# Modulation in chunks of two channel tiles, with the first head's projections and gates formed tile by tile between them

## The chip, the cores and the metric

The kernel runs on one core of one Trainium2 chip. The metric is device time in microseconds (us) of one execution; a kernel's time is the median of its runs. Engines are named as in the profile: PE (TensorE), PEld (its weight loads), DVE (VectorE), ACT (ScalarE), POOL (GpSimd) and SP (SyncE, which here only issues DMAs).

## The reference, cut to what matters

One layer of a hybrid trunk over 128 context tokens and 1024 latent tokens (1152 in all, nine token tiles of 128), with 1024 channels (eight channel tiles of 128). What the change touches is the beginning:

```python
shift, scale, gate = jnp.split(silu(c) @ w_mod + b_mod, 3, axis=-1)   # c_ctx for the context tokens, c for the latents
h = rmsnorm(x, p['norm_w']) * (1 + scale) + shift
proj = h @ p['w_in']
qkv, z_a, x_b, z_b, gate_cols = jnp.split(proj, [OFF_QKV, OFF_ZA, OFF_XB, OFF_ZB], axis=-1)
q, k, v = l2norm(...silu(conv(qkv))...)                                # 8 heads of 128
alpha_f, beta_f, alpha_b, beta_b = jnp.split(gate_cols, 4, axis=-1)    # 32 columns
g = -exp(a_log) * softplus(alpha + dt_bias);  beta = sigmoid(beta)     # both directions
# then per head: chunked gated delta rule in both directions, RG-LRU branch, merge, output projection
```

(The first line is shortened from the model code that feeds the layer; the rest is the reference's.) All products have float32 accuracy. For the large ones the kernel splits each operand into a high and a low part of type fp32r and adds three products (high by high, high by low, low by high).

## The kernel before, in words

The program is written engine by engine, by hand; semaphores alone order the engines, and each engine works its own list strictly in order. `front_stage` (L153 on) holds everything up to the end of the eight DeltaNet heads, `tail_stage` the rest. The change touches `front_stage` alone, before and just inside head 0.

**x and modulation.** For each of nine token tiles t, SP loads x (L337, `x_load`, three buffers, so a load waits until tile t-3 is normalised), ACT squares it with a row sum (L649), POOL forms the reciprocal root (L450, L452), ACT scales it (L643), PE transposes it in eight blocks into two PSUM banks (L893 to L896), and DVE copies it to `xt`, channels on partitions (L1205). Between the transposes of tiles 0 to 7, PE forms the modulation: silu(c) for channel tile t (128 x 2, the stationary operand) by 2048 columns of `w_mod` (the moving one), four matmuls per t (L881), summed over t in four PSUM banks. So shift and scale exist only after all eight. Then DVE copies the four 2x512 rows out (L1210), PE transposes them (L900), DVE forms `gain` and `shift` for all eight channel tiles (L1217 to L1220), and the modulated rows begin.

**Rows and the first block.** For each channel tile k, DVE writes x * gain + shift (L1233), ACT rounds it to the high part (L660), DVE subtracts for the low part (L1226). PE, in step with k, forms the first 128-column block of `w_in` (the key of head 0): three token groups of 384 columns by three products, nine matmuls per k (L912, L913, L917), and the 32 gate columns: again nine matmuls per k, with the 128x32 gate weights stationary and 384 tokens moving (L922, recorded as L124 to L126). The gates thus come out with columns on partitions; ACT copies them out (L663) and PE turns them with nine small transposes (L928).

**The second and third block, and the gates.** PE then forms blocks 1 (query) and 2 (value) of head 0 with `project(j, g)` (L848), 24 matmuls for each of three groups. Among them stand the gate transposes, the cumulative sums of the decays (L940) and the turning of their results (L947). DVE works the gates (L1241 to L1277), starts the convolutions of head 0 (`conv`, L1146 and L1148, one multiply and three multiply-adds per row), and copies the decay rows out (L1280); SP stores them and loads them back broadcast over the partitions (L322, `decay_in`); POOL masks them (L467); ACT takes their exponential (L612). Between two convolutions DVE forms the rate of the other branch (`softplus` of lambda and two scalings, L1282 to L1285).

**Head 0.** PE begins with the sums of squares of q (L963, after ACT's `square_q`, L607), turns the key (L864), and forms the key products (L970), the last two groups after ACT has copied the key out (L714). DVE needs the row sums of ACT's squares (L710) before it goes on (L1294), and from there runs to the end of the triangular solve (L1341, L1343, 31 steps, L1353); ACT then places blocks (L761), for which PE's L1032 waits. The projections of the next head are placed by hand between PE's steps.

**Filler.** `keep_busy` (L129) issues matmuls whose result nobody reads: 9 at the start (L875), 23 before the first block (L902), 10 before head 0 (L952).

The weights go through one staging buffer `wst` (`load(j)`, L316), ACT's `high(j)` and POOL's `low(j)` make the two parts, and `load(j)` waits until the low part of block j-1 is done.

## Time and profile before

| | us |
|---|---|
| median of 3 runs | 1642.02 |
| lowest and highest | 1639.0, 1642.07 |
| profiled execution, its own time | 1642.41 |
| its span in the trace | 1640.6 |
| PE busy in the span | 1591.3 (97%) |
| DVE, ACT, POOL busy | 1001.6, 805.4, 348.2 |
| mean granted TensorE clock | 0.992 of full |

Busy PE time comes from records whose ends are modelled: a matmul of 384 columns shows 335 ns, but the next starts about 173 ns later. The pace is therefore read from starts. A matmul of two float32 operands leaves two records.

### The profile page before, as it was taken

To read this page: it belongs to the slowest core of one execution; us is meant where nothing else is said; L and a number is where in the kernel's file an instruction comes from. 1 tells how busy PE (TensorE), PEld (TensorE's weight loads), DVE (VectorE), ACT (ScalarE), POOL (GpSimd) and SP (SyncE) were. 2 spreads that over 40 slices of the span, in tenths; PEclk is the share of its full clock that TensorE was granted. 3 is DMA by queue.
4 is the path that set the end of the run, shared out by engine and by line. 5 is a ranking of instruction groups with operands and counts; after the bars stand their busy time and mean duration, and the time that the engine had idled before them with its cause. 6 is when DMAs were issued, how large, how long until landed. Compare 5 with 4: busy or idle time off the path is not lost. (4 is left out here: it accounts for less than half of the span.)

```text
span 1640.6 us, 25151 instructions
## 1 busy us (share of the span) xinstructions
PE 1591.3 (97%) x9994; PEld 1512.5 (92%) x9994; DVE 1001.6 (61%) x1729; ACT 805.4 (49%) x1655; POOL 348.2 (21%) x272
## 2 busy tenths in 40 slices
PE   8989999999999999999999999999999999999997
PEld 3789999999999999999969999999999999999886
DVE  2647869597786959778664475663574641244444
ACT  4336474655748465564724764566466630221211
POOL 1122322121232212122211222221221211143110
PEclk9999999999999999999999999999999999999999
DMA  9121112012221201212240121212122262344123
GB/s 322 54 61 27 72 30 95 21 41 71 57 72 30 96 20 41 72 57 71 69 137 17 47 77 51 79 55 74 53 75 60 75 199 74 102 153 136 54 77 128
DMA packets 115855, 127.27 MB, mean 78 GB/s; under 512 B 6461, under 2 KB 97430, under 8 KB 115738
## 3 DMA queue, kind: packets, MB, share of 16 engines
q1 hardware_dynamic: 115594, 125.60, 23.8%
q8 instruction: 79, 1.29, 0.3%
q14 instruction: 38, 0.31, 0.1%
q10 hardware_dynamic: 144, 0.07, 0.0%
HBM read 105.56 MB, written 20.09 MB: 77 GB/s over the span
## 5 line engine op out<-in xcount | busy, mean ns | idle before, releaser
L124 PE MATMUL mb<-h_hi,w_hi 128*128 128x384 f32 x1088 | 365.3, 336 | 6.8 <-PEq L156 3.4
L125 PE MATMUL mb<-h_lo,w_hi 128*128 128x384 f32 x1088 | 364.7, 335 | 0.0
L126 PE MATMUL mb<-h_hi,w_lo 128*128 128x384 f32 x1088 | 364.5, 335 | 0.0
L124 PE MATMUL db<-h_hi,w_hi 128*128 128x384 f32 x808 | 283.6, 351 | 4.9 <-ACT padded_rows L668 2.2
L126 PE MATMUL db<-h_hi,w_lo 128*128 128x384 f32 x808 | 271.4, 336 | 0.0
L125 PE MATMUL db<-h_lo,w_hi 128*128 128x384 f32 x808 | 271.4, 336 | 0.0
L1665 POOL TENSOR_TENSOR w_lo<-w,w_hi 128x1024 fp32r<-128x1024 f32 x47 | 126.9, 2702 | 475.2 <-ACT w_hi L1692 475.2
L124 PEld LDWEIGHTS mb<-h_hi,w_hi 128*128 128x128 f32 x1088 | 205.1, 188 | 8.3 <-issue 4.7
L125 PEld LDWEIGHTS mb<-h_lo,w_hi 128*128 128x128 f32 x1088 | 205.1, 189 | 0.0
L126 PEld LDWEIGHTS mb<-h_hi,w_lo 128*128 128x128 f32 x1088 | 205.1, 189 | 0.0
L124 PEld LDWEIGHTS db<-h_hi,w_hi 128*128 128x128 f32 x808 | 152.9, 189 | 5.8 <-ACT d_kq L663 2.6
L125 PEld LDWEIGHTS db<-h_lo,w_hi 128*128 128x128 f32 x808 | 153.1, 189 | 0.0
L126 PEld LDWEIGHTS db<-h_hi,w_lo 128*128 128x128 f32 x808 | 152.4, 189 | 0.0
L1692 ACT ACTIVATE w_hi<-w 128x1024 fp32r<-128x1024 f32 x47 | 49.6, 1058 | 122.0 <-PE mb L126 76.5
L1938 DVE SCALAR_TENSOR_TENSOR l_tg<-l_tg,d_dt 128x1155 f32<-128x1155 f32 x16 | 36.5, 2324 | 96.4 <-ACT l_tg L1759 96.4
L811 ACT ACTIVATE d_vn<-db,d_nc 128x128 f32<-128x128 f32 x144 | 45.0, 363 | 96.8 <-DVE d_vk L1403 94.0
L1343 DVE TENSOR_TENSOR d_qg<-d_qg 128x31 f32<-128x31 f32 (+15 forms) x248 | 85.2, 344 | 8.5
L1341 DVE TENSOR_TENSOR d_qg<-d_qg 128x31 f32<-128x31 f32 (+15 forms) x248 | 84.6, 341 | 7.3
L1042 PEld LDWEIGHTS db<-d_w,d_u 128*96 128x96 f32 x864 | 77.1, 165 | 0.3
L1042 PE MATMUL db<-d_w,d_u 128*96 128x32 f32 (+2 forms) x864 | 76.7, 248 | 0.0
L518 POOL COPY d_w<-d_qg 32x288 f32<-32x288 f32 x32 | 22.6, 707 | 225.2 <-DVE d_qg L1353 223.8
L460 POOL TENSOR_TENSOR w_lo<-w,w_hi 128x1024 fp32r<-128x1024 f32 x20 | 47.6, 2380 | 102.8 <-ACT w_hi L542 102.8
(303 smaller groups left out, 2955.8 us busy)
## 6 DMA issues: line engine op xcount, KB each, us to landing
w<-in_w_in SPq DMA_DIRECT2D x48, 512.0 KB, 4.0
d_dt<-decay_rows SPq DMA_DIRECT2D x16, 576.0 KB, 5.5
d_qg<-decay_rows SPq DMA_DIRECT2D x16, 512.0 KB, 7.6
w<-in_w_gate SPq DMA_DIRECT2D x16, 512.0 KB, 3.9
branch_a<-d_kq SPq DMA_DIRECT2D x8, 576.0 KB, 3.2
branch_b<-l_z SPq DMA_DIRECT2D x8, 576.0 KB, 2.8
merge_gates_b<-l_gates SPq DMA_DIRECT2D x8, 576.0 KB, 5.2
m_in<-merge_gates_b SPq DMA_DIRECT2D x8, 576.0 KB, 3.8
```

What stands on the lines that cost most here:

```text
L124: pe.matmul(out, hi, rhi, start=(k == 0), stop=False)
L125: pe.matmul(out, hi, rlo, start=False, stop=False)
L126: return pe.matmul(out, lo, rhi, start=False, stop=(last and stop))
L460: pool.tensor_tensor(wlo[:, j % 2], wst[:, :, :], whi[:, j % 2].bitcast(F32), ALU.subtract).then_inc(S["w_lo"], 1)
L518: pool.tensor_copy(dst[bs, ns, bs], src_[bs, :].rearrange("p (b n) -> p n b", n=B)[:, ns, :]).then_inc(S[sem], 1)
L811: act.activation(vn[:, d, :], bank[3 + 2 * d][:, 0:P], ACT.Copy, scale=ncol[:, d, t:t + 1]).then_inc(S["vn"], 1)
L1042: mm = pe.matmul(back_bank(level, d, p)[0:3 * B, (t - t0) * width:(t - t0 + 1) * width], umat[:, d * NT + t, rc[d]], vinv(d, t)[:, col:col ...
L1341: link(dve.tensor_tensor(prod, amat[:, k * B + k + 1:(k + 1) * B].unsqueeze(2).broadcast_to([P, n, m]), xmat[:, k * B:k * B + m].unsqueeze ...
L1343: link(dve.tensor_tensor(low_rows, low_rows, prod, ALU.add))
L1665: pool.tensor_tensor(wlo_of(item), wst[:, slot(j)], whi_of(item).bitcast(F32), ALU.subtract).then_inc(S["w_lo"], 1)
L1692: act.activation(whi_of(item), wst[:, slot(j)], ACT.Copy).then_inc(S["w_hi"], 1)
L1938: dve.scalar_tensor_tensor(out=tg[:, 2 * d + 1, :], in0=tg[:, 2 * d + 1, :], scalar=1.0, in1=xc, op0=ALU.add, op1=ALU.mult).then_inc(S["p" ...
```

## The change: what it does

- The modulation is formed in four chunks; chunk c gives shift and scale for channel tiles 2c and 2c+1 alone. It sums over all eight input tiles, 256 + 256 columns of `w_mod` for each, eight matmuls per chunk. `w_mod` comes in 32 DMAs of 256 KB into eight buffers. Chunk 0 is formed between the transposes of token tiles 3 to 6, chunk 1 after those of tile 8, chunk 2 after channel tile 1, chunk 3 after channel tile 3. Each chunk has one row copy, four small transposes and three small DVE operations of its own.
- Between the chunks, for each channel tile, PE forms blocks 0 and 1 of `w_in` together (18 matmuls of 384 columns) and the gates.
- The gates are formed by tokens: for each of nine token tiles the 128x128 tile of h is stationary and the 128x32 gate weights move, three products each, 27 matmuls per channel tile, straight into the layout that the nine transposes made before. Those and ACT's copy go.
- DVE reads the gates after the last channel tile; block 1 is by then done, and only block 2 is left among the cumulative sums.
- x has four buffers; all four loads go out first, and the other loads are in a new order. The first block's weights are rounded during tile 5, their low part comes from DVE after tile 6. Block 2's weights have buffers of their own.
- The `softplus` of lambda moves into head 0, ahead of the transposes of the solve.
- `keep_busy` and its three uses are gone. Before head 0 PE waits for the copy of the decay rows.

The diff, cut to its core:

```diff
-        x = (flat_of(w1)[:, 0:D], flat_of(w1)[:, D:2 * D], flat_of(w2)[:, 0:D])
+        x = (flat_of(w1)[:, 0:D], flat_of(w1)[:, D:2 * D], flat_of(w2)[:, 0:D], flat_of(w2)[:, D:2 * D])
...
@@ SP
-            x_load(0)
-            x_load(1)
+            for t in range(NX):
+                x_load(t)
             sp.wait_ge(S["rows_zero"], 1)
...
+            for c, r, src, n in sources[0:9]:
+                sp.dma_start(rows_in_[r:r + n, c, :], src).then_inc(S["rows_in"], 16)
+            mod_load(0, 0)
+            x_load(4)
+            mod_load(0, 1)
...
+            load(0)
+            x_load(5)
+            mod_load(0, 2)
...
+            x_load(8)
+            mod_load(1, 1)
+            load(1)
+            mod_load(1, 2)
+            mod_load(1, 3)
...
+            for q in range(PARTS):
+                mod_load(2, q)
             load(2)
+            for q in range(PARTS):
+                mod_load(3, q)
             load(3)
...
@@ PE
-            keep_busy(pe, bank[7][:, 0:P], ident, 9)
             pe.wait_ge(S["silu_c"], 1)
+
+            def modulation(c, q):
+                n = c % 2 * PARTS + q
+                pe.wait_ge(S[f"wm{n}"], 32 * (c // 2 + 1))
+                if q == 0 and c >= 2:
+                    pe.wait_ge(S["mod"], 3 * c)
+                for k in range(2):
+                    mm = pe.matmul(bank[0 if c == 1 else 1][0:2, :], sc[:, :, 2 * q + k],
+                                   wmod[n][:, k].rearrange("p a n -> p (a n)"), start=(q == 0 and k == 0),
+                                   stop=(q == PARTS - 1 and k == 1))
+                mm.then_inc(S["mod_part"], 1)
...
+                if 3 <= t < 7:
+                    modulation(0, t - 3)
+                elif t == 7:
+                    mod_turned(0)
+            for q in range(PARTS):
+                modulation(1, q)
             pe.wait_ge(S["x_e"], NT)
-            pe.wait_ge(S["mod"], 2)
             pe.wait_ge(S["par_done"], 1)
...
+            pe.wait_ge(S["mod_row"], 2)
+
+            def first_blocks(k):
+                pe.wait_ge(S["h_hi"], k + 1)
+                for j in range(2):
+                    low_done(pe, j)
+                    for g in range(NG):
...
+                        pe.matmul(b[:, 0:GW], whi[:, j, k, :], R.hhi[:, k, ts], start=(k == 0), stop=False)
+                        pe.matmul(b[:, 0:GW], wlo[:, j, k, :], R.hhi[:, k, ts], start=False, stop=False)
+                pe.wait_ge(S["h_lo"], k + 1)
...
+                for t in range(NT):
+                    ts = slice(t * P, (t + 1) * P)
+                    at = bank[0][:, t * 4 * H:(t + 1) * 4 * H]
+                    pe.matmul(at, R.hhi[:, k, ts], wghi[:, k, :], start=(k == 0 and t == 0), stop=False,
+                              skip_group_check=True)
+                    pe.matmul(at, R.hhi[:, k, ts], wglo[:, k, :], start=False, stop=False, skip_group_check=True)
+                    mm = pe.matmul(at, R.hlo[:, k, ts], wghi[:, k, :], start=False, stop=(k == KT - 1),
+                                   skip_group_check=True)
+                return mm
+
             for k in range(KT):
-                pe.wait_ge(S["h_hi"], k + 1)
...
+                mm = first_blocks(k)
+                if k % 2 == 0 and k < KT - 2:
+                    mod_turned(k // 2 + 1)
+                elif k in (1, 3):
+                    for q in range(PARTS):
+                        modulation(k // 2 + 2, q)
             mm.then_inc(S["g_mm"], 1)
-            pe.wait_ge(S["g_row"], NG)
-            project(1, 0)
...
-            project(1, 1)
-            project(1, 2)
+            project(2, 0)
             pe.wait_ge(S["consts_in"], 16 * len(consts))
             pe.wait_ge(S["gates_raw"], 3)
...
-            project(2, 0)
+            project(2, 1)
             pe.wait_ge(S["cum_exp"], 2)
...
-            project(2, 1)
             project(2, 2)
-            keep_busy(pe, bank[5][:, 0:P], ident, 10)
+            pe.wait_ge(S["dec_copy"], 1)
             pe.wait_ge(S["cum_exp"], 4)
@@ DVE
+                if t == 6:
+                    dve.wait_ge(S["w_hi"], 1)
+                    dve.tensor_tensor(wlo[:, 0], wst[:, :, :], whi[:, 0].bitcast(F32), ALU.subtract).then_inc(S["w_lo"], 1)
+                elif t == 7:
+                    gains(0)
...
-                if k:
+                if k % 2:
+                    if k == 1:
+                        mod_rows(1)
                     low_rows(k - 1)
-            low_rows(KT - 1)
-
-            dve.wait_ge(S["g_t"], 1)
+                    low_rows(k)
+                    if k < KT - 1:
+                        if k > 1:
+                            mod_rows(k // 2 + 1)
+                        gains(k // 2 + 1)
+
+            dve.wait_ge(S["g_mm"], 1)
...
             conv(0, 2, range(TAPS))
-            softplus(sct[:, :], lu[:, :], lw[:, :], lr[:, :], ll[:, :], lam, -1.0)
...
             conv(0, 1, range(TAPS))
...
                 link(ins)
+                if h == 0:
+                    softplus(sct[:, :], lu[:, :], lw[:, :], lr[:, :], ll[:, :], lam, -1.0)
...
                 dve.wait_ge(S["u"], (h + 1) * 2 * NG)
```

`mod_rows(c)` waits for the chunk's last matmul and copies its 2x512 row; `mod_turned(c)` is four small transposes of it; `gains(c)` forms gain and shift for two channel tiles.

## Rows read from the trace of the kernel before

**Rows 1.** The page: the span, and its busy times by engine.
```profile
span 1640.6 us, 25151 instructions
PE 1591.3 (97%) x9994; PEld 1512.5 (92%) x9994; DVE 1001.6 (61%) x1729; ACT 805.4 (49%) x1655; POOL 348.2 (21%) x272
```

**Rows 2.** Timeline, 0 to 62 us: start, duration, engine, line, instruction, count.
```profile
3.04 4.21 PE L132 MATMUL db<-ident 128*128 128x128 f32 x18
...
18.56 1.09 PE L894 MATMUL db<-ident,d_dt 128*128 128x128 f32 x8
...
19.58 1.88 PE L881 MATMUL db<-d_kn,silu_c 128*2 128x512 f32 x4
...
50.59 2.46 DVE L1210 COPY d_k<-db 2x512 f32<-2x512 f32 x4
50.73 1.09 PE L894 MATMUL db<-ident,d_w 128*128 128x128 f32 x8 [1.45 <-DVE xt L1205]
...
61.67 0.42 PE L912 MATMUL db<-h_hi,w_hi 128*128 128x384 f32 x1
```

**Rows 3.** Groups by line, ACT, first 130 us: busy, mean ns, idle before, releaser.
```profile
L649 ACT ACTIVATE d_u<-d_w 128x1024 f32<-128x1024 f32 x9 | 9.5, 1057 | 23.2 <-DMA d_w<-in_x_sample 21.9 <-DMA d_w<-in_x_prompt 1.3
L643 ACT ACTIVATE d_w<-d_w,rstd 128x1024 f32<-128x1024 f32 x5 | 5.7, 1135 | 0.0
```

**Rows 4.** Busy times in a stretch; the last three are clock, DMA share, GB/s.
```profile
9.00:32.00 23.00, 22.31 (x71) 6.55 (x72) 5.15 (x8) 8.79 (x13) 2.97 (x8) 1.00 0.91 317
```

**Rows 5.** Timeline, PE: the last gate matmul of the first block's loop.
```profile
86.76 0.33 PE L126 MATMUL db<-h_hi,wg_lo 128*32 128x384 f32 x1
```

**Rows 6.** Groups by line and shape, PEld, first 100 us: weight loads, mean ns.
```profile
L912 PEld LDWEIGHTS db<-h_hi,w_hi 128*128 128x128 f32 x24 | 4.5, 188 | 0.5
L124 PEld LDWEIGHTS db<-h_hi,wg_hi 128*32 128x32 f32 x24 | 2.6, 107 | 1.0
```

**Rows 7.** Timeline, PE: streams of short matmuls in heads 0 and 1.
```profile
175.68 2.14 PE L1032 MATMUL db<-d_w,d_u 128*128 128x96 f32 x18
...
181.78 3.17 PE L1042 MATMUL db<-d_w,d_u 128*96 128x32 f32 x36
...
222.48 2.07 PE L963 MATMUL db<-ident,d_cb 128*128 128x1 f32 x18
```

**Rows 8.** Timeline from the gates to the cumulative sums, 95 to 108 us.
```profile
95.21 0.74 PE L928 MATMUL db<-ident,d_kq 32*128 32x32 f32 x9
...
95.99 0.46 DVE L1241 COPY d_qg<-db 128x288 f32<-128x288 f32 x1 [19.65 <-PE db L928]
...
101.72 0.46 DVE L1273 TENSOR_TENSOR d_qg<-d_qg,exp_a_log 128x72 f32<-128x72 f32 x2
...
103.14 4.34 DVE L1148 SCALAR_TENSOR_TENSOR d_k<-padded_rows,par,d_k 128x1155 f32<-128x1155 f32 x3
...
106.52 1.45 PE L940 MATMUL db<-d_qg,d_kq 128*128 128x72 f32 x12
```

**Rows 9.** Timeline from the decay rows into head 0, 112 to 136 us.
```profile
112.66 0.69 DVE L1280 COPY d_kq<-db 72x512 f32<-72x512 f32 x1 [5.18 <-PE db L947]
...
118.43 0.25 DVE L1261 RECIPROCAL lam_r<-lam_w 128x16 f32<-128x16 f32 x1
...
120.05 0.17 DVE L1285 TENSOR_SCALAR lru_rate<-silu_c_tanh 128x16 f32<-128x16 f32 x1
...
122.06 3.70 POOL L467 TENSOR_SCALAR_AFFINE_SELECT d_dt<-d_dt 128x1152 f32<-128x1152 f32 x2 [9.95 <-DMA d_dt<-decay_rows]
...
123.89 1.36 PE L963 MATMUL db<-ident,d_cb 128*128 128x1 f32 x11 [0.69 <-ACT d_cb L607]
...
125.06 5.37 ACT L612 ACTIVATE d_dt<-d_dt,gates 128x128 f32<-128x128 f32 x18
...
135.27 0.17 DVE L1294 TENSOR_SCALAR d_ssk<-d_ssk 128x9 f32<-128x9 f32 x1 [6.76 <-ACT d_kn L710]
...
135.81 1.60 PE L970 MATMUL db<-d_k 128*128 128x128 f32 x12 [0.80 <-ACT d_kn L714]
```

**Rows 10.** Timeline, ACT: what PE's L1032 of head 0 waits for.
```profile
172.91 1.51 ACT L761 ACTIVATE d_w<-d_qg 32x288 f32<-32x288 f32 x2 [2.78 <-DVE d_qg L1353]
```

More of the change, by code:

```diff
@@ L126, in split_product @@
     return pe.matmul(out, lo, rhi, start=False, stop=(last and stop))
-def keep_busy(pe, out, ident, n):
-    for _ in range(n):
-        pe.matmul(out, ident, ident, start=True, stop=True)
 def evacuate_lru(act, rows, src, q):
@@ L173, in front_stage @@
         cb_ = sb("d_cb", [P, CONV])
+        with nc.sbuf_tensor("v_w_hi", [P, KT, P], F32R) as vhi, nc.sbuf_tensor("v_w_pad", [P, P], F32), \
+                nc.sbuf_tensor("v_w_lo", [P, KT, P], F32R) as vlo:
+            pass
         kn = sb("d_kn", [P, NT, P])
@@ new lines, in _ @@
+            mod_load(0, 0)
+            x_load(4)
+            mod_load(0, 1)
+            for c, r, src, n in sources[9:18]:
+                sp.dma_start(rows_in_[r:r + n, c, :], src).then_inc(S["rows_in"], 16)
+            load(0)
+            x_load(5)
+            mod_load(0, 2)
+            for dst, src in small:
+                sp.dma_start(dst, src).then_inc(S["small_in"], 16)
+            x_load(6)
+            mod_load(0, 3)
+            x_load(7)
+            mod_load(1, 0)
+            x_load(8)
@@ L482, in clear_tail @@
                 pool.memset(temp[:, 0:BB].rearrange("p (b n) -> p b n", n=B)[:, :, NI:B], 0.0).then_inc(S["tz"], 1)
-            low(0)
             low(1)
@@ L547, in evac @@
                 for at, lo, hi in spans(g):
[L548 removed]
+                    ins = act.activation(dst[:, at:at + hi - lo], proj_bank(gi)[:, lo:hi], ACT.Copy)
                 ins.then_inc(S["proj_out"], 1)
@@ L691, in _ @@
             act.activation(flat(G_EXPALL), bank[4][:, 0:NI * H], ACT.Exp).then_inc(S["cum_exp"], 1)
-            evac(1, 2, row_of(-1, 2))
+            evac(2, 0, row_of(-1, 1))
+            silu(0, 0)
+            evac(2, 1, row_of(-1, 1))
             high(3)
-            silu(0, 0)
-            for g in range(NG):
-                evac(2, g, row_of(-1, 1))
+            evac(2, 2, row_of(-1, 1))
             silu(0, 2)
@@ L924, in _ @@
-            mm.then_inc(S["g_mm"], 1)
-            pe.wait_ge(S["g_row"], NG)
-            project(1, 0)
-            for t in range(NT):
-                mm = pe.transpose(bank[0][:, t * 4 * H:(t + 1) * 4 * H], gfeat[:, t * P:(t + 1) * P],
-                                  R.ident[0:4 * H, 0:4 * H])
-            mm.then_inc(S["g_t"], 1)
-            project(1, 1)
-            project(1, 2)
+            pe.wait_ge(S["mod_row"], 2)
[3 more added lines that the diff above has]
+                    low_done(pe, j)
+                    for g in range(NG):
+                        ts = slice(g * GW, (g + 1) * GW)
+                        b = proj_bank(j * NG + g)
+                        pe.matmul(b[:, 0:GW], whi[:, j, k, :], R.hhi[:, k, ts], start=(k == 0), stop=False)
+                        pe.matmul(b[:, 0:GW], wlo[:, j, k, :], R.hhi[:, k, ts], start=False, stop=False)
+                pe.wait_ge(S["h_lo"], k + 1)
+                for j in range(2):
+                    for g in range(NG):
+                        ts = slice(g * GW, (g + 1) * GW)
+                        mm = pe.matmul(proj_bank(j * NG + g)[:, 0:GW], whi[:, j, k, :], R.hlo[:, k, ts], start=False,
+                                       stop=(k == KT - 1))
+                        if k == KT - 1:
+                            mm.then_inc(S["proj_mm"], 1)
+                for t in range(NT):
[7 more added lines that the diff above has]
+                return mm
@@ L1193, in _, with mod_rows, gains @@
             xt = R.xt
+            def mod_rows(c):
+                dve.wait_ge(S["mod_part"], PARTS * (c + 1))
+                if c:
+                    dve.wait_ge(S["mod_t"], c)
+                dve.tensor_copy(modrow, bank[0 if c == 1 else 1][0:2, :]).then_inc(S["mod_row"], 1)
+            def gains(c):
+                dve.wait_ge(S["mod_t"], c + 1)
+                ks = slice(2 * c, 2 * c + 2)
+                per_k = lambda v: v[:, :, ks].rearrange("p a k -> p k a")
+                par_k = lambda at: R.par[:, at + 2 * c:at + 2 * c + 2].unsqueeze(2).broadcast_to([P, 2, 2])
+                mod_of = lambda i: bank[1][:, 4 * i:4 * i + 4].rearrange("p (k a) -> p k a", a=2)
+                dve.tensor_tensor(per_k(gain), mod_of(1), par_k(B_SCALE), ALU.add).then_inc(S["mod"], 1)
+                dve.tensor_tensor(per_k(shift), mod_of(0), par_k(B_SHIFT), ALU.add).then_inc(S["mod"], 1)
+                dve.wait_ge(S["mod"], 3 * c + 2)
+                dve.tensor_tensor(per_k(gain), per_k(gain), par_k(PA_NORM), ALU.mult).then_inc(S["mod"], 1)
+                dve.wait_ge(S["mod"], 3 * c + 3)
             for t in range(NT):
                 if t == 7:
+                    mod_rows(0)
                     dve.wait_ge(S["rows_t"], 1)
```

145 lines of the change are left out of this document (48 added, 97 removed).

## The prediction

> **What bounds the kernel now.** I read the page first: PE is busy 97% of a span of 1640.6 us [rows 1]. So from head 0 to the end the order on PE sets the pace, and whatever delays or advances the start of head 0 should move the end by as much. Then I read the timeline of the first 175 us, to find what that start waits for. Three stretches matter.
>
> In the first, to 61.67 us [rows 2], PE forms the modulation between the transposes. A pair of modulation matmuls (four records) keeps PE for 4 x 0.43 = 1.72 us, and its row shows 1.88 with the drain; eight transposes take 1.09. ACT is not the limit: it waited 23.2 us in all for x to land [rows 3], while the DMA queues moved 317 GB/s at a 0.91 share [rows 4]. The last x tile is transposed at 50.73, and then 61.67 - 50.73 = 10.9 us pass in row copies, small transposes, gains and the first rows, before the first projection starts.
>
> In the second, 61.67 to 86.9 [rows 2, 5], 144 matmuls of 384 columns, half of them for gates, go at (86.93 - 61.67)/144 = 0.175 us. PE is the limit there.
>
> In the third, blocks 1 and 2 of head 0 and the gates' own chain run side by side. Two milestones count. M1 is 106.52, when the cumulative sums start and blocks 0 and 1 are done [rows 8]. M2 is 135.27, when DVE gets the row sums of the key (L1294) [rows 9]; from there the solve runs 39 us to the placed blocks at 174.42, the end of L761's two copies [rows 10], and PE is at L1032 at 175.68 [rows 7]. So in head 0 that chain has only about 1.2 us of slack: a later M2 is a later end.
>
> **The change, part by part.** All times are those of the profiled execution; with its 1642.41 us it lies 0.4 above the median of 1642.02, so a difference found here is added to the median.
>
> Start of the loop. The modulation as a whole costs PE the same 27.5 us (32 matmuls before and after), but only two chunks of four (13.8 us) now stand before the first projection; chunks 2 and 3 (2 x 6.9) move into the loop. The lower end for the start: ACT needs 1.06 + 0.19 + 1.14 = 2.4 us per x tile [rows 3], from about 5 us nine tiles give 26.5; last transposes and their wait 2, chunk 1 6.9, its row copy 0.6: 36. The upper end: x no faster than before, 50.7 + 1.1 + 6.9 + 0.6, and the rest hidden: 59. Between them I take the data: until x tile 8 lands, nine x tiles, five parts of `w_mod` and one weight block must have moved, 15 x 0.52 = 7.9 MB, at 317 GB/s 25 us plus 2 for the start; until chunk 1 is complete 10 MB, 34 us, in time for its matmuls. After x tile 8, ACT still has 3.5 us; on DVE the weight's low part, the chunk-0 row, the parameters and tile 7's copies now queue ahead of PE's last transposes (1.3 + 0.6 + 1.0 + 1.3), so these start near 33.8. Plus 1.1, 6.9 and 0.6 gives 42.5. The filler is gone and PE has only transposes until tile 3. At the lower clock level (1.2 GHz), where it began before (18 records in 4.21 us, 0.234 each, against 0.11 later [rows 2, 7]), some of chunk 0 costs double: 0.5 more. Start: 43, so 18.7 earlier than before. The 10.9 us of small steps are hidden beside chunk 1 and cost nothing; their cover is 6.9 us of PE work, and beyond it only the one row copy shows. SP's many small loads are ahead of x tiles 4 to 8, one reason why I don't go nearer to 36.
>
> (The Trainium skill says in "TensorE: Matmul & The Clock Gate", Part 4, that transposes do not count as PE work for the faster clock. By that rule all work before chunk 0 is at 1.2 GHz, about the same 0.5 to 1 us; PE waits there for x anyway.)
>
> Length of the loop. Blocks 0 and 1 are 144 matmuls at 0.175: 25.2 us. The gates were 72 matmuls of 384 columns with 32-column weights; they are now 27 x 8 = 216 matmuls that stream 32 columns each, but every one loads 128 columns of weights. No row has an fp32r matmul this short. The nearest rows are streams with a 128-column load and a short moving part: 18 of one column take (2.07 - 0.25)/17 = 0.107 us each, 18 of 96 columns (2.14 - 0.27)/17 = 0.110 [rows 7]; they are bound by the load. These are float32; that fp32r loads at the same pace I read from the load records: 188 ns for 128 columns and 107 for 32, 0.84 ns for each further column [rows 6]; 128 columns make 0.107 us. I take 0.109: 216 x 0.109 = 23.5 us, where 72 x 0.175 = 12.6 stood: **the gates cost 10.9 us more**, less 0.7 for the nine transposes. The ends: 0.065, the pace of the nine transposes of L928 ((0.74 - 0.22)/8 [rows 8]), is 9.5 us less; 0.175, as if each were a full matmul, 14 more. Two chunks 13.8; three times four small transposes, by L928's pace with a switch, 0.5 each: 1.5; switches 0.8. Sum 25.2 + 23.5 + 13.8 + 1.5 + 0.8 = 64.8. The waits inside hide: gains for tiles 2c and 2c+1 are formed while PE works one more channel tile (6.1 us) or a chunk, against some 4 to 5 us of DVE and ACT work. If that cover were gone, three waits of about 3 us would come.
>
> So the loop ends at 43 + 64.8 = 107.8, with blocks 0 and 1 and the gates done. M1 before was 106.52: so far **1.3 us later**. The accounts balance so: 18.7 gained at the start, and 6.3 of waits and slow clock that go (block 1's 72 matmuls and the nine transposes needed 72 x 0.175 + 0.7 = 13.3 of the 19.6 us from 86.9 to 106.5), and 0.7 for the nine transposes, pay for 13.8 of modulation, 10.9 of gates and 2.3 of small steps.
>
> From the gates to head 0. Before, the gates were ready at 95.95, while block 1 was still being formed, and their chain of 6.2 us on DVE and ACT (95.99 to 102.18 [rows 8]) was hidden. Now they are ready only at the end of the loop. Counted from there: 6.2 for that chain (PE fills 4.2 with a group of block 2 and idles 2), 1.25 for the sums, 4.15 for the next group, 0.4 for turning, 0.8 for the decay-row copy: 12.8. ACT's evacuations and DVE's first convolution (5.3, ending at about 11.7) fit inside. From the end of that copy to POOL's mask it was 122.06 - 113.35 = 8.7 us of DMA out and in [rows 9]; mask of the first direction 1.85; 18 exponentials 5.4; then silu of the value and the squares, 135.27 - 130.43 = 4.8. Sum 33.6, so M2 = 107.8 + 33.6 = 141.4 against 135.27: **6.1 later**. Before, ACT's `square_q` and the mask came together at 123.8; now ACT is done with `square_q` 20.5 to 21.5 after the gates and the mask at 23.4 is what ends last.
>
> Head 0. The `softplus` of lambda (118.43 to 120.22, 1.8 us [rows 9]) now lies inside DVE's chain: 1.8 - 1.2 of slack = 0.6. PE idles some 4 us before head 0 and again before M2, with the filler gone; if it restarts at 1.2 GHz, the work after M2 loses about 1.7 us on PE. The two run side by side, so I take the larger: 1.7. The new wait for the decay-row copy is met long before. Sum 6.1 + 1.7 = 7.8: **1642.0 + 8 = 1650 us**.
>
> **The rivals.** A measurement of this kernel can tell about 0.2%, 3.3 us, from no change.
>
> (1) The forecast: load-bound gates, late chain. With the start between 39 and 47 and the clock losses 0 to 3.4, it gives 1644 to 1657. Chance 0.6.
>
> (2) Faster: short gate matmuls don't pay the full load. If the array keeps the h tile between two products that share it, or loads it faster, the pace is 0.04 to 0.065, and everything after the loop comes 216 x 0.056 = 12 us earlier: 1638. It decides from a pace of 0.072 down (8/216 below 0.109); under 0.057 the gain can be measured. Against it: before, two consecutive products with the same weights both show a load, and the load records grow with the columns [rows 6]. Chance 0.17. (The Trainium skill, same page, section "Weight-path perf modes — Fast Weight Load (FWL) and DoubleRow": a load of 128 weight columns whose type is not FP32 takes a faster path, measured at about twice the speed. Read so that fp32r counts as not FP32, it says this rival, with an estimated pace of 0.055 and 1638; the 188 ns of [rows 6] speak against it.)
>
> (3) The front hides more: x and data arrive at ACT's pace, start at 37 and no slow clock: 1642 + 8 - 6 - 1.7 = 1642.3. For it: ACT had 23 us of idle. Against it: SP's order and DVE's queue. Chance 0.13.
>
> (4) The gate matmuls count too little for the clock, and part of them and what follows runs at 1.2 GHz: half of them at 0.215 is 12 us more, 1662. Against it: 36 records that move 32 columns each ran at 0.083 [rows 7], the full level. Chance 0.1.
>
> **How the numbers follow.** The likeliest is (1): 1650. The range 1637 to 1658 takes in (1), (3) and most of (2). Faster by over 0.2%: most of (2), 0.14. Within 0.2%: (3), the rest of (2) and the low edge of (1), 0.19. Slower: 0.67.
>
> **What would show it.** First projection near 43; eight loop rounds of 6.1 us with 27 short matmuls at 0.109 and 188 ns loads; loop end near 108; masks near 129; L1294 near 141; PE idle before L963. Wrong if the short matmuls pace under 0.08, if the loop starts before 38, or if head 1 begins no later than before.

## The result, and the profile of the changed kernel

| | before | after |
|---|---|---|
| median of the runs beside each other | 1642.05 us (1639.0 to 1644.54, 4 runs) | 1665.62 us (1663.61 to 1666.44, 4 runs) |
| profiled execution | 1642.41 | 1665.01 |
| its span | 1640.6 | 1663.2 |
| mean granted clock | 0.992 | 0.985 |

The changed kernel is slower: the ratio is 1.0143, 95% interval 1.0123 to 1.0162, which is 23.6 us. The forecast was 1650 with a range up to 1658: the sign was right, the size was not (+8 was forecast), and the result lies outside the range. Of all executions below one fell into a slower state (1992.46 us at a granted clock of 0.745, a kernel with both filler and earlier decay transposes), and ratios and clocks leave it out.

The page of the changed kernel, its span and its busy times by engine, beside [rows 1]:

```profile
span 1663.2 us, 25292 instructions
PE 1603.5 (96%) x10045; PEld 1527.4 (92%) x10045; DVE 1007.3 (61%) x1739; ACT 803.7 (48%) x1652; POOL 347.1 (21%) x271
```

PE is still the busy engine, so the question stays where head 0's start was held up. Each step has its milestone in the trace:

| milestone | before | forecast | after |
|---|---|---|---|
| first projection starts | 61.67 | 43 | 46.56 |
| loop with the gates ends | 87.1 | 107.8 | 119.2 |
| M2, row sums of the key on DVE | 135.27 | 141.4 | 154.26 |
| first step of head 0's solve on DVE | 145.15 | about 153 | 165.85 |
| row sums of the key of head 1 on DVE | 227.43 | about 235 | 247.24 |
| total (median) | 1642 | 1650 | 1665.6 |

Against the forecast, 3.6 us were lost at the start, 7.8 in the loop (it took 72.6, not 64.8) and 1.5 from its end to M2. From M2 to head 1 the changed kernel lost 0.8 where 1.7 was forecast: it is 19.0 us late at M2 and 19.8 at the row sums of head 1. The two profiled executions differ by 22.6 us, so 2.8 come behind head 1; the medians differ by 23.6.

**The start.** The timeline of the changed kernel from 31 to 47 us, rows of PE, DVE and POOL (start, duration, engine, line), beside [rows 2]:

```profile
33.63 0.41 PE L903 MATMUL db<-ident,d_kq 2*128 2x2 f32 x4 [0.27 <-DVE d_kq L1233]
35.79 1.62 PE L917 MATMUL db<-ident,d_dt 128*128 128x128 f32 x8 [1.75 <-DVE xt L1259]
37.33 2.99 PE L894 MATMUL db<-d_q,silu_c 128*2 128x512 f32 x4
41.88 3.60 PE L894 MATMUL db<-d_k,silu_c 128*2 128x512 f32 x8
46.56 0.41 PE L938 MATMUL db<-h_hi,w_hi 128*128 128x384 f32 x1 [1.08 <-DVE d_kq L1233]
...
31.78 1.22 DVE L1263 TENSOR_TENSOR w_lo<-w,w_hi 128x1024 fp32r<-128x1024 f32 x1
34.45 1.29 DVE L1259 COPY xt<-db 128x512 f32<-128x512 f32 x2
38.72 2.41 DVE L1267 TENSOR_TENSOR wg_lo<-d_w,wg_hi 128x256 fp32r<-128x256 f32 x1
...
38.50 2.34 POOL L475 TENSOR_TENSOR w_lo<-w,w_hi 128x1024 fp32r<-128x1024 f32 x1 [6.78 <-ACT w_hi L557]
```

The last x tile's transposes wait 1.75 us for tile 7's copies, which stand on DVE behind the weight's low part, the row copy and the parameters. That is the queue that the forecast named, but they start at 35.79 and not at 33.8. Then PE is at its lower clock until 39.3: eight transposes take 1.62 for 1.09, four modulation matmuls 2.99 for 1.88. From there on PE works without a gap up to the row copy. PE was slow at the very start too: the transposes of the first four x tiles took 1.94 to 1.97 us each, those from 23.44 on 1.10. Tile 3 was normalised at 15.45 and transposed only at 18.87; by tile 5 (26.21 and 26.66) x was what PE waited for again, so little of that can have reached the loop.

**The loop.** Groups by line and shape on PE, 40 to 135 us (busy, mean ns of one), the answer to [rows 6, 7]:

```profile
L938 PE MATMUL db<-h_hi,w_hi 128*128 128x384 f32 x48 | 20.1, 419 | 1.1 <-DVE d_kq L1233 1.1
L955 PE MATMUL db<-wg_hi,h_lo 128*128 128x32 f32 x72 | 19.1, 265 | 0.0
L954 PE MATMUL db<-wg_lo,h_hi 128*128 128x32 f32 x72 | 19.0, 264 | 0.0
L952 PE MATMUL db<-wg_hi,h_hi 128*128 128x32 f32 x72 | 18.3, 255 | 0.0
L944 PE MATMUL db<-h_lo,w_hi 128*128 128x384 f32 x48 | 10.3, 353 | 0.0
```

A record of 264 ns overlaps its neighbours; the pace is read from starts. The timeline of PE where the seventh round's gates end and the eighth round begins:

```profile
111.02 0.26 PE L952 MATMUL db<-wg_hi,h_hi 128*128 128x32 f32 x1
111.13 0.26 PE L954 MATMUL db<-wg_lo,h_hi 128*128 128x32 f32 x1
111.24 0.34 PE L955 MATMUL db<-wg_hi,h_lo 128*128 128x32 f32 x1
111.42 0.67 PE L938 MATMUL db<-h_hi,w_hi 128*128 128x384 f32 x1
111.88 0.52 PE L939 MATMUL db<-h_hi,w_lo 128*128 128x384 f32 x1
112.20 0.52 PE L938 MATMUL db<-h_hi,w_hi 128*128 128x384 f32 x1
...
114.44 0.46 PE L939 MATMUL db<-h_hi,w_lo 128*128 128x384 f32 x1
114.74 0.34 PE L938 MATMUL db<-h_hi,w_hi 128*128 128x384 f32 x1
114.92 0.33 PE L939 MATMUL db<-h_hi,w_lo 128*128 128x384 f32 x1
```

Short matmuls start every 0.11 us (111.02, 111.13, 111.24): the term of 0.109 was right, and rival 2 is gone. But behind the last of the 27 the pace changes: 384 columns take 0.32 us in place of 0.175, up to 114.4. No engine is waited for. The clock shows it, in the windows of the changed kernel (length of the stretch, busy time and instructions of PE, PEld, DVE, ACT, POOL, then the granted clock PEclk, DMA share, GB/s):

```profile
46.50:53.00 6.50, 6.44 (x48) 6.44 (x49) 2.23 (x2) 0.00 (x0) 0.00 (x0) 1.00 1.12 347
53.00:60.90 7.90, 7.90 (x49) 7.88 (x47) 5.08 (x9) 2.23 (x2) 0.00 (x0) 0.78 0.13 41
74.90:82.00 7.10, 7.10 (x32) 7.08 (x32) 5.07 (x9) 2.22 (x2) 0.00 (x0) 0.60 0.00 1
82.00:92.00 10.00, 10.00 (x33) 3.21 (x32) 0.00 (x0) 0.00 (x0) 0.00 (x0) 0.83 0.01 2
92.00:100.00 8.00, 8.00 (x56) 7.52 (x55) 1.46 (x6) 0.00 (x0) 0.00 (x0) 1.00 0.00 0
110.00:119.20 9.20, 9.20 (x60) 9.20 (x60) 0.00 (x0) 2.64 (x8) 0.00 (x0) 0.81 0.00 1
```

Four falls to 1.2 GHz lie in the loop, 53.1 to 56.5, 73.7 to 80.2, 83.8 to 87.2 and 111.3 to 114.5, together some 17 us at half level, which loses 8.5. Each begins in the last short matmuls of a round or just behind them (rounds 1, 3, 4 and 7 of the eight), while PE was busy without a gap (7.90 of 7.90). 72.6 - 8.5 = 64.1: at full clock the loop is about as long as forecast.

**The tail.** The timeline from the end of the loop into head 0, all engines, the answer to [rows 8, 9]:

```profile
118.95 0.26 PE L955 MATMUL db<-wg_hi,h_lo 128*128 128x32 f32 x1
125.32 1.53 PE L975 MATMUL db<-d_qg,d_kq 128*128 128x72 f32 x12 [1.84 <-issue]
130.89 0.60 PE L982 MATMUL db<-ident,gates 128*72 128x128 f32 x4
133.04 6.32 DVE L1182 SCALAR_TENSOR_TENSOR d_q<-padded_rows,par,d_q 128x1155 f32<-128x1155 f32 x3
133.13 3.55 POOL L475 TENSOR_TENSOR w_lo<-w,w_hi 128x1024 fp32r<-128x1024 f32 x1 [23.29 <-ACT w_hi L557]
141.03 3.93 POOL L481 TENSOR_SCALAR_AFFINE_SELECT d_dt<-d_dt 128x1152 f32<-128x1152 f32 x2 [4.35 <-DMA d_dt<-decay_rows]
141.90 0.77 PE L997 MATMUL db<-ident,d_cb 128*128 128x1 f32 x3 [6.25 <-ACT d_cb L622]
142.76 1.28 ACT L627 ACT_TABLE_LOAD   x1 [1.00 <-POOL d_dt L481]
144.05 5.37 ACT L627 ACTIVATE d_dt<-d_dt,gates 128x128 f32<-128x128 f32 x18
154.26 0.17 DVE L1343 TENSOR_SCALAR d_ssk<-d_ssk 128x9 f32<-128x9 f32 x1 [8.01 <-ACT d_kn L720]
165.85 0.19 DVE L1395 TENSOR_TENSOR d_qg<-d_qg 128x31 f32<-128x31 f32 x1
```

As forecast, the gates' chain is now bare: 6.1 us from the last gate matmul to the sums, of which PE idles 1.84. From the decay transposes (130.89) to M2 it takes 23.4 us, before 135.27 - 112.02 = 23.3. So once the sums are late, all is late by the same amount. The forecast had 22.0 for this stretch: it let the exponentials follow the mask of the first direction, 1.85 us after the mask's start, but ACT loads a table first (1.28 us), and from the mask's start to the exponentials it is 3.0 us in both kernels (144.05 - 141.03; 125.06 - 122.06).

**Head 0.** The solve starts 20.7 us late, 1.7 more than M2, because the softplus (1.8 us) stands between. The row sums of head 1, here the same line in the kernel before and after, are only 19.8 late:

```profile
227.43 0.17 DVE L1294 TENSOR_SCALAR d_ssk<-d_ssk 128x9 f32<-128x9 f32 x1 [2.69 <-ACT d_kn L710]
247.24 0.17 DVE L1343 TENSOR_SCALAR d_ssk<-d_ssk 128x9 f32<-128x9 f32 x1 [2.69 <-ACT d_kn L720]
```

So slack behind the solve took up 0.9 of the 1.7, and the softplus costs about 0.8.

### The profile page after: what moved, and what is told of

Read it like the earlier page. It is cut to its first block and busy times, and to the rows that moved or that the text cites. A ratio compares the mean times of both kernels' runs of the same rounds, so it can differ in the third digit from the quotient of the medians.

```text
span 1663.2 us, 25292 instructions
## 1 busy us (share of the span) xinstructions
PE 1603.5 (96%) x10045; PEld 1527.4 (92%) x10045; DVE 1007.3 (61%) x1739; ACT 803.7 (48%) x1652; POOL 347.1 (21%) x271
## 5 line engine op out<-in xcount | busy, mean ns | idle before, releaser
L124 PE MATMUL db<-h_hi,w_hi 128*128 128x384 f32 x760 | 266.3, 350 | 0.8 <-DVE d_k L1416 0.8
L126 PE MATMUL db<-h_hi,w_lo 128*128 128x384 f32 x760 | 255.0, 335 | 0.0
L125 PE MATMUL db<-h_lo,w_hi 128*128 128x384 f32 x760 | 254.7, 335 | 0.0
L1719 POOL TENSOR_TENSOR w_lo<-w,w_hi 128x1024 fp32r<-128x1024 f32 x47 | 126.4, 2691 | 475.4 <-ACT w_hi L1746 475.4
L124 PEld LDWEIGHTS db<-h_hi,w_hi 128*128 128x128 f32 x760 | 143.4, 189 | 1.0 <-DVE d_k L1416 1.0
L125 PEld LDWEIGHTS db<-h_lo,w_hi 128*128 128x128 f32 x760 | 143.4, 189 | 0.0
L126 PEld LDWEIGHTS db<-h_hi,w_lo 128*128 128x128 f32 x760 | 143.0, 188 | 0.0
L563 ACT ACTIVATE padded_rows<-db 128x128 f32<-128x128 f32 (+1 forms) x80 | 30.7, 422 | 73.5 <-PE db L126 61.7
```

Source lines behind the costliest of these rows:

```text
L124: pe.matmul(out, hi, rhi, start=(k == 0), stop=False)
L125: pe.matmul(out, hi, rlo, start=False, stop=False)
L126: return pe.matmul(out, lo, rhi, start=False, stop=(last and stop))
L563: ins = act.activation(dst[:, at:at + hi - lo], proj_bank(gi)[:, lo:hi], ACT.Copy)
L1719: pool.tensor_tensor(wlo_of(item), wst[:, slot(j)], whi_of(item).bitcast(F32), ALU.subtract).then_inc(S["w_lo"], 1)
```

## The experiments

Theory: the miss is the clock, which falls because of the short gate matmuls; beside it stand the price of their pace (+11, forecast), the bare gates' chain and the softplus in head 0's chain. Rival: the falls belong to the chunks, whose matmuls have only two output rows.

The kernels ran in several sessions. Beside the changed kernel the kernel before had a median of 1642.05, beside the first four experiments 1640.34, beside the others 1641.64 to 1642.14. Where two kernels of different sessions are compared, their distances from the kernel before are therefore given as well.

**Gates by rows in the changed kernel.** All three groups share one bank, by weights of 96 columns that are zero outside their group:

```diff
-                for t in range(NT):  # three products, R.hhi/R.hlo[:, k, ts] stationary, 32 columns moving
+                for g in range(NG):
+                    at, ws = bank[0][0:96, 0:GW], slice(64 - 32 * g, 160 - 32 * g)
+                    pe.matmul(at, wghi[:, k, ws], R.hhi[:, k, ts], ...)
+                    pe.matmul(at, wghi[:, k, ws], R.hlo[:, k, ts], ...)
+                    pe.matmul(at, wglo[:, k, ws], R.hhi[:, k, ts], ...)
```

> The changed kernel with the gates by rows again: the gate weights stationary (96 columns, zeros around each group's 32), tokens moving 384 at a time, 72 matmuls in the place of 216; one eviction and 3 transposes behind the loop as they were needed before. Theory (the loop is long because 216 short matmuls cost 0.111 us each, and because the clock falls behind each of their stretches): 216 x 0.111 = 24.0 us go, 72 x 0.175 = 12.6 come, the 17 us at half clock in the loop go (8.5 us lost), the way over the eviction costs about 1.5: loop of about 53 us for 72.6, in all about -18 us against the changed kernel, 1647. Rival (the clock falls for another reason, such as the chunks' modulation matmuls): only the pace comes back, -10, 1656, and the windows of the loop still show half clock.

Measured: 1649.19 us, ratio 1.0053 (1.0039 to 1.0066) to the kernel before. Against the changed kernel 16.4 us are back between the medians, 14.7 by the distances from the kernel before (23.6 and 8.9). The loop took 53.7 us (46.10 to 99.8, 53 expected) at a granted clock of 1.00.

**The same instructions, interleaved.** After each long matmul one or two of the short ones:

```diff
                         pe.matmul(b[:, 0:GW], whi[:, j, k, :], R.hhi[:, k, ts], start=(k == 0), stop=False)
+                        gate(3 * i, False)
+                        gate(3 * i + 1, False)
                         pe.matmul(b[:, 0:GW], wlo[:, j, k, :], R.hhi[:, k, ts], start=False, stop=False)
+                        gate(3 * i + 2, False)
```

> The changed kernel with its 27 short gate matmuls of a channel tile set between the 18 of 384 columns, instead of behind them; the same instructions otherwise. Theory (the clock falls because the short ones stand together): no half clock in the loop, 0.111 us a short matmul still (their weight load is behind nothing), loop 64 us for 72.6, in all -8 to -9, about 1657. Rival 1 (the clock follows the share of loading over the whole round, not its order): falls remain, no change, 1665. Rival 2 (a load is hidden under a long neighbour): the short ones cost less than 0.111 too, loop below 60, under 1652.

Measured: 1655.9 us, ratio 1.0088 (1.0061 to 1.0114). The loop went from 45.83 to 110.7: 64.9 us, where the forecast said 64.8. A long and a short matmul together took 0.29 us, 0.175 and 0.115, so no load hides. Windows in this kernel, the same stretches in which the changed kernel fell (same columns as above):

```profile
46.00:58.00 12.00, 12.00 (x90) 11.96 (x90) 7.08 (x11) 2.23 (x2) 0.00 (x0) 1.00 0.82 253
66.00:78.00 12.00, 12.00 (x92) 11.96 (x90) 5.47 (x10) 2.23 (x2) 0.00 (x0) 1.00 0.00 1
78.00:88.00 10.00, 10.00 (x40) 4.29 (x39) 0.68 (x1) 0.00 (x0) 0.00 (x0) 1.00 0.01 2
```

The chunks' matmuls are all in it, with the same operands and in the same places between the rounds, and the clock stays at 1.00. The rival falls: the chunks alone don't bring the falls. Without one instruction more or less, 9.7 us are back between the medians, 8.0 by the distances from the kernel before, 7.7 of them in the loop. This is not one lucky execution: the mean granted clock of the four was 0.989 to 0.992, in the changed kernel's four 0.982 to 0.987.

**Gates by tokens alone, in the kernel before.** No chunks, no second block in the loop; evictions and transposes of the gates gone:

```diff
-                    mm = split_product(pe, bank[5 + g][0:4 * H, 0:GW], wghi[:, k, :], wglo[:, k, :], ...)
+                    pe.matmul(at, R.hhi[:, k, ts], wghi[:, k, :], ...)   # at: 32 columns of bank 5, per token tile
+                    pe.matmul(at, R.hhi[:, k, ts], wglo[:, k, :], ...)
+                    mm = pe.matmul(at, R.hlo[:, k, ts], wghi[:, k, :], ...)
```

> The kernel before with one part of the change alone: gates formed by tokens (216 short matmuls into bank 5, evictions and transposes of the gates gone). Theory: 216 x 0.111 = 24.0 in the place of 72 x 0.175 = 12.6 is +11.4; the clock falls behind the stretches as in the changed kernel, +8; the evictions and transposes that go give back about 1: +18, about 1660. Rival (the falls belong to the chunks): +10, about 1652, loop at full clock.

Measured: 1666.36 us, ratio 1.015 (1.0127 to 1.0174); 26.0 above the kernel before beside it, where the theory gave 18. One part of the change costs as much as the whole. Windows of its loop (60.39 to 118.8):

```profile
60.00:66.00 6.00, 5.59 (x40) 5.30 (x41) 5.65 (x7) 3.33 (x4) 0.00 (x0) 1.00 0.20 61
66.00:90.00 24.00, 24.00 (x115) 24.00 (x114) 11.05 (x14) 4.99 (x5) 0.00 (x0) 0.58 0.00 1
90.00:94.00 4.00, 4.00 (x33) 4.00 (x32) 0.00 (x0) 0.00 (x0) 0.00 (x0) 0.93 0.00 0
94.00:119.00 25.00, 25.00 (x107) 25.00 (x106) 0.14 (x1) 2.26 (x5) 3.96 (x2) 0.50 0.02 4
```

From 66 us nearly all of it is at half level, though PE has no idle time. A short matmul then takes 0.21 us.

**The softplus back** (between the second and the third convolution, as before):

```diff
             conv(0, 2, range(TAPS))
+            softplus(sct[:, :], lu[:, :], lw[:, :], lr[:, :], ll[:, :], lam, -1.0)
+            ...
             conv(0, 1, range(TAPS))
...
-                if h == 0:
-                    softplus(...)
```

> The changed kernel with the decay rate's softplus back ahead of the third convolution of head 0, instead of in head 0's chain behind the u tiles. It took 1.8 us of VectorE there (159.93 to 161.73). Theory: the convolution ahead of head 0 is not the last to come (squares and the clock set L997's start), so the step is hidden again and head 0's solve starts 1.7 us earlier: -1.7, 1664. Rival: VectorE's row of convolutions is on the path, and the same 1.8 us is only moved: 0.

Measured: 1664.1 us, 1.5 under the changed kernel's median but 23.8 above the kernel before beside it, as the changed kernel's 23.6; the interval of its ratio to the kernel before (1.0106 to 1.0149) overlaps that of the changed kernel, so the total alone does not settle it. The trace does: from M2 to the solve 165.05 - 155.16 = 9.9 us, in the changed kernel 165.85 - 154.26 = 11.6, so the step was on the path to the solve with 1.7. From M2 to the row sums of head 1 it is 92.2 us, as in the kernel before, and 93.0 in the changed kernel: 0.8 arrives there.

**One product of three** (the two gate products with low parts are left out):

```diff
-                    pe.matmul(at, R.hhi[:, k, ts], wglo[:, k, :], ...)
-                    mm = pe.matmul(at, R.hlo[:, k, ts], wghi[:, k, :], ...)
```

> A cost probe: the changed kernel with one of the three gate products (high parts by high parts) and the two with low parts left out, so that 72 short matmuls stand in stretches of 9 where 216 stood in stretches of 27. Theory: 144 x 0.111 = 16.0 us of pace go, and with stretches of 1 us the clock stays full, which gives back the 8.5 us lost in the loop: -24, about 1641. Rival (the falls are not tied to the stretches' length): -16, about 1649.

Measured: 1640.33 us, ratio 0.9991 (0.9975 to 1.0007): 25.3 for the 24 that pace and clock together were to give. Its loop took 48.6 us, 24.0 less than 72.6, and its clock from 46 to 100 us is 1.00, that of the changed kernel 0.87. (It leaves out two products of three, so it is a probe and not a way to form the gates.)

**Interleaved gates in the kernel before.** Each long matmul is followed by three short ones:

```diff
                         pe.matmul(bank[2 + g][:, 0:GW], w[:, 0, k, :], R.hhi[:, k, ts], ...)
+                        for n in range(3):
+                            gate(6 * g + 3 * i + n, False)
```

> The kernel before with gates by tokens, as in the run of that part alone (whose loop of 58.4 us was at half clock from 66 to 124), but with each channel tile's 27 short matmuls set three by three between its 9 long ones. Theory A (what counts is that short matmuls stand together for microseconds): full clock, loop of 72 x 0.175 + 216 x 0.111 = 36.6 us, total about +11 against the kernel before, 1653. Rival B (what counts is their share of the time: 24.0 of 36.6 us here, 24.0 of 63 in the changed kernel): the clock falls here all the same, as in the run with the stretches, 1660 or more. In the changed kernel interleaving kept the clock full, which both allow.

Measured: 1673.13 us, ratio 1.0192 (1.0162 to 1.0221). The interval just overlaps that of the kernel with the stretches, but the loop is longer, 65.1 us for 58.4. Windows of its loop (61.22 to 126.3):

```profile
60.00:64.00 4.00, 4.00 (x35) 4.00 (x34) 3.93 (x7) 1.33 (x3) 0.00 (x0) 1.00 0.07 19
64.00:68.00 4.00, 4.00 (x25) 4.00 (x25) 3.93 (x6) 2.26 (x2) 0.00 (x0) 0.74 0.00 0
80.00:90.00 10.00, 10.00 (x43) 10.00 (x43) 0.00 (x0) 0.00 (x0) 0.00 (x0) 0.50 0.01 2
100.00:110.00 10.00, 10.00 (x43) 10.00 (x44) 0.00 (x0) 0.00 (x0) 0.00 (x0) 0.50 0.00 0
```

After the first rounds it is at 1.2 GHz to the end. So the theory that only standing together counts is refuted. The order decided in the changed kernel, where 18 long matmuls go with 27 short ones and chunks lie between; with 9 long ones to 27 short the order helps nothing.

**What the chunked order is worth with gates by rows.** Four kernels build on the first experiment. First, in the last channel tile the gates come first and their eviction and transposes follow at once, while the second block's share of the last two tiles is formed behind them:

```diff
+            for k in range(KT):                      # j = 1 is left out of the last two k
+                js = (0,) if k >= KT - 2 else (0, 1)
+                if k == KT - 1:
+                    gate_rows(k).then_inc(S["g_mm"], 1)
...
+            mm.then_inc(S["g_t"], 1)                 # three transposes of the evicted gates
+            for k in (KT - 2, KT - 1):
+                first_highs(k, (1,))
+                first_lows(k, (1,))
             project(2, 0)
```

> The kernel with the gates by rows once more, and the last two channel tiles reordered: the gates' last matmuls first, their eviction and transposes right behind, and the 18 + 18 matmuls of the second block's last two channel tiles and its successor's first group after them. In the run with the gates by rows TensorE stood idle for 4.7 us ahead of the decay sums, whose input left VectorE 9.1 us after the last gate matmul, and the clock was at half from 107 to 113. Theory (that wait is what the chunked order lost against the kernel before, which hides the gates' chain behind 12.6 us of projections): the sums start at 104.5 in the place of 109.1, the decay transposes 5.5 us later in the place of 7.8 (full clock): -6.8, about 1642. Rival (the next thing, the two groups still to be projected or VectorE's convolutions, is as late): -2, 1647.

Measured: 1644.71 us, ratio 1.0013 (1.0002 to 1.0024): -4.5 between the medians, -6.3 by the distances from the kernel before (8.9 and 2.6), where -6.8 was expected. The wait ahead of the sums was the one sought (here in the kernel of the first experiment, with PE idle for 4.69 us):

```profile
109.08 1.31 PE L987 MATMUL db<-d_qg,d_kq 128*128 128x72 f32 x5 [4.69 <-issue]
```

It is 1.19 now, and the sums start 107.63 - 48.06 = 59.6 us after the first projection, in the kernel of the first experiment 63.0. The solve starts 99.7 us after it, there 105.7: 6.0 gained. In this execution the first projection was late itself (48.06), which hid 2 us in the profile.

Second, the softplus goes back and a quarter of chunk 1 goes into PE's gap ahead of the last x tile:

```diff
                 elif t == 7:
                     mod_turned(0)
+                    modulation(1, 0)
-            for q in range(PARTS):
+            for q in range(1, PARTS):
                 modulation(1, q)
```

> The gates-first kernel with the softplus of the decay rate back ahead of the third convolution (-1.8 in head 0's chain) and one quarter of the second chunk's matmuls moved into TensorE's 1.75 us of idle time ahead of the last x tile's transposes (-1.5 at the start of the loop). Theory: both are on the path: -3.3 against the gates-first kernel, near 1639, level with the kernel before or a little under it. Rival: the start is bound by the operands' chain on VectorE and ScalarE, and only the softplus counts: -1.8.

Measured: 1643.87 us, ratio 1.0009 (1.0 to 1.0019): -0.8, where -3.3 was expected; that is within the scatter. In the profiles the first projection starts at 44.0 to 45.9 (five executions of kernels with this start, those below among them) in place of 45.8 to 48.1 (six with the old one), in the mean 44.8 and 46.7; the solve starts at 144.95. The total did not show all of that. Part of the reason stands in head 0: from the first projection to the row sums of head 1 it is 182.1 us, 181.1 with the gates early alone, so of 1.9 us at the start 1.0 was lost again by there, and the softplus gave nothing that lasts (M2 to these sums 93.6 us, 93.0 without the step; 92.2 in the changed kernel with the softplus back). What takes it up was not traced.

Third, filler and earlier decay transposes, first both, then each alone, then both again:

```diff
-            project(2, 1)
+            project(2, 1, range(0, 3))
             pe.wait_ge(S["cum_exp"], 2)
...
             mm.then_inc(S["dec_t"], 1)
+            project(2, 1, range(3, KT))
             project(2, 2)
             pe.wait_ge(S["dec_copy"], 1)
+            keep_busy(pe, bank[5][:, 0:P], ident, 40)
```

> The same with 40 filler matmuls ahead of head 0's sums of squares, and the decay transposes after 3 of the 8 channel tiles of the group they stood behind. Theory: the 3.97 us of sums at half clock become 2.1, but the path to head 0's inverse norms goes over the decays, so they gain nothing; the decays' masks come up to 2.6 us earlier, but ScalarE takes the squares of q first: -1 in all. Rival: the decay chain alone is the path, -2.6.

> The kernel with gates first and the softplus back, with the 40 filler matmuls ahead of head 0 alone (without the earlier decay transposes). The run with both gained 5.1 us where 1 was expected. Theory: full clock for head 0's sums and the transposes, projections and products behind them is worth 2.5 us, 1641.4. Rival (the filler gains nothing, since the way goes over the decays): 0, 1643.9.

> The kernel with gates first and the softplus back, with the decay transposes earlier alone (without the filler). Theory: the masks come 2.6 us earlier, the decays wait for the squares of q, and half of it arrives: -1.5, 1642.4. Rival (the decay chain alone is the path): -2.6, 1641.3.

> The kernel with filler and earlier decay transposes once more, unchanged, in more rounds: each alone gained 0.5 and 1.4 us on the kernel with gates first, both together 5.1. Theory (the two lie on two ways to the same point, so only together they move it: the squares' sums at full clock and the decays): 1638 to 1640 again, under the kernel before by 0.1 to 0.2%. Rival (the 1638.8 was the draw of later clock falls): 1641 to 1642, level with the kernel before.

Measured: both 1638.81 us, ratio 0.998 (0.997 to 0.999); filler alone 1643.35, 1.0006 (0.9997 to 1.0016); decay transposes alone 1642.5, 1.0006 (0.9996 to 1.0016); both again 1640.24, 0.9991 (0.998 to 1.0002). From the first projection to the solve it is 99.1 us without either, 98.2 and 98.6 with one, 97.4 and 97.9 with both. At the solve the two gains are small and simply add up: 0.8 and 0.5. The solve is too early a place to read them, though. To the row sums of head 1 it is 182.1 us without either, 182.1 with the filler, 181.7 with the decay transposes, 179.7 and 180.2 with both. In the profile with the filler alone a clock fall lies in head 0 (0.66 from 182 to 187 us), which costs 1.6; without it that kernel would be at 180.5. So by the traces the filler is worth about 1.6 (with it M2 to these sums is 92.2 us, without it 93.6), the decay transposes 0.4, both 1.9 to 2.4: still a sum, and the idea of two ways that must move together is not borne out there. The totals gave 0.5 and 1.4 alone and 5.1 the first time with both (3.1 the second, by the distances from the kernel before). Part of that is where clock falls landed; the mean granted clock was 0.991 to 0.993 in the ten executions without either, 0.994 to 0.996 with the filler and 0.991 to 0.999 in those with both. Whether the filler has a part in that is open. The two medians of this version lie 1.4 and 3.3 us under the kernel before; the second time the interval reaches 1. It is level with it or 0.1 to 0.2% better, with gates by rows, not by tokens.

## Why the prediction was wrong, step by step

- **The sign and its reasons** held. The modulation was only moved, not saved; the gates' short matmuls cost more than the gates by rows did; and the gates' chain, hidden before, is now bare.
- **The pace of the short matmuls**: right, 0.111 us for 0.109. Rival 2 (kept or faster weights) is refuted by the starts above.
- **The loop, 64.8 us**: 72.6. This is the step that failed: the sum took every matmul of the loop at the full level, 216 x 0.109 and 144 x 0.175. The granted clock was at half for some 17 us of it. That was rival 4, "the gate matmuls count too little for the clock", which had 0.1 and the price +12. Its effect is what happened, with 8.5 us in the loop. It was argued away with 36 records of 32 columns at 0.083 us, at full level [rows 7]. Those follow a long stretch of dense work and last 3 us; they show that such a stream can run at the full level, not that eight of them in 70 us leave it there. With the same instructions interleaved the loop took 64.9 and the total was 8.0 to 9.7 less, so it is shown that the falls hang on these matmuls and their order, and what they cost. By what rule the clock falls is not shown.
- **The start, 43 us**: 46.56, a term of the sum that was too small. DVE's queue ahead of the last x tile was named, but ended 2 us later than summed, and 1.6 came from the lower clock between 35.8 and 39.3. Over six executions with this start it lay between 45.8 and 48.1, so the 43 was wrong and not unlucky.
- **From the loop to M2, 33.6**: 35.1, right in its structure. Of the 1.5 us, 1.2 are the table load ahead of the exponentials, which the sum left out, though its own rows show 3.0 us from mask to exponentials and not 1.85 [rows 9]. The sums start 6.1 after the last gate matmul, as summed. The decay chain (DMA, mask, exponentials) ended last and not `square_q`, which was at 141.76, 0.7 after the mask's start. The second convolution took 6.32 for 4.34 beside POOL's low part; ahead of the decays that cost little.
- **Head 0, +1.7**: +0.8 (19.0 late at M2, 19.8 at the row sums of head 1). The forecast took the larger of two costs, 1.7 for a slow PE over 0.6 for the softplus behind its slack. PE did start head 0 at half level (L997 took 3.97 us for 2.14), but its cost did not arrive; the 0.6 was nearly right. That the solve is 1.7 later than M2 agrees with the 1.7 of the forecast by chance.
- **Behind head 0**: the forecast had nothing there. Two clock falls of the changed kernel, at 681 to 684.5 and near 1466 to 1469 (0.55 and 0.56 in these windows), lose 1.6 and 1.7, and the kernel before has none there; the rest of the way gave 0.5 back. From the row sums of head 1 to those of head 7 it is 571.9 us in seven of the fourteen profiles and 573.5 in the other seven, so one such fall comes or does not. What sets that is open.

In sum: 3.6 + 7.8 + 1.5 - 0.9 + 2.8 = 14.8, and 1.0 by which the medians lie further apart than the profiled executions: 15.8, the miss of 23.6 - 7.8. The range ended at 1658 and left rival 4 outside with its 0.1. One row of a 3 us stream in other surroundings was weak evidence against it, and it alone kept that chance so low.

## What to carry to other kernels

A matmul that moves few columns costs its weight load (0.11 us here for 128 columns), and swapping operands so that the small side moves can make it dearer: 216 of these for 72 of 384 columns. It also changes the clock of its neighbours, so that the price of such a stream is to be read from a stream that recurs among the same neighbours. Where a chain is hidden behind projections, a fusion that lets all of them end together lays it bare; do the part that a chain waits for first. And read what a step gave where the engines have met again: in head 0's solve the softplus was worth 1.7 us, at head 1 it was 0.8.

## What the runs showed of the hardware that was not expected

- TensorE fell to 1.2 GHz while it was busy without any gap. In the kernel before with gates by tokens, the granted clock was 0.58 from 66 to 90 us and 0.50 from 94 to 119, with PE and its loads busy throughout; in the changed kernel four falls of 3.2 to 6.5 us.
- The fall reached the long matmuls behind the short ones: 0.32 us each at 111.88 to 114.4 for 0.175, and modulation matmuls at 83.8 too.
- The same instructions in another order kept 1.00 in the changed kernel; in the kernel before, interleaving the gates left 0.50 for over 50 us. What the clock goes by was not settled.
- A wait was not needed for a fall: in the window 66 to 90 us of the kernel before with gates by tokens PE is busy 24.00 of 24.00 us at 0.58. The Trainium skill, "TensorE: Matmul & The Clock Gate", section "HAM oscillation — how this bites in real kernels", tells of a clock that falls back in waits for data between groups of matmuls; these rows show the same with no wait at all.
- DVE and POOL slow each other: `wg_lo` took 2.41 us beside POOL's low part (2.34 at the same time, begun 0.2 us earlier) and ended 0.3 us after it, at 41.13; it took 0.41 in the kernel with gates by rows, where POOL began 0.3 us later than DVE. Three passes of a convolution took 6.32 for 4.34 beside a low part that itself took 3.55 for 2.41.
